# Plain writes for the gate scatters of the first head in a PEER decoder step

## The reference

```python
q = (tb @ wq).reshape(PEER_BLOCK, PEER_HEADS, 2, PEER_QHALF)
sc = jnp.einsum('thpd,hpnd->thpn', q, keys)
s1, i1 = lax.top_k(sc[:, :, 0], PEER_TOPK)
s2, i2 = lax.top_k(sc[:, :, 1], PEER_TOPK)
...
top_s, top_p = lax.top_k(cand, PEER_TOPK)
eidx = jnp.take_along_axis(cidx, top_p, axis=-1)
g = jax.nn.softmax(top_s, axis=-1)
act = jax.nn.gelu(jnp.einsum('td,thkd->thk', tb, u_tab[eidx]))
w = (g * act)
return jnp.einsum('thk,thkd->td', w, v_tab[eidx])
```

## Time and profile before

| | |
|---|---|
| Runs before the change | 3567.2, 3569.97, 3570.47 us, median 3569.97 |
| Span of the profiled execution | 3562.4 us |
| The profiled execution's own time | not listed apart; the median lies 7.6 us above the span |
| Mean granted TensorE clock | 0.976 of full speed |
| Scatters at the edited line | 384, median 1547 ns, from 700.5 to 1429.8 us |
| Barrier between the two blocks | about 1445.3 us |

### The profile page before, as it was taken

One profiled execution on the slowest core, in us unless ns is written; L12 is line 12 of the kernel. 1 busy time (PEld: TensorE's weight loads), 2 busy tenths in 40 slices (PEclk: granted clock), 3 DMA queues, 4 the chain that ended last, 5 costly groups with the idle time before them and its releaser, 6 DMA issues.

```text
span 3562.4 us, 41298 instructions
## 1 busy us (share of the span) xinstructions
PE 3364.8 (94%) x12551; PEld 1749.8 (49%) x12551; DVE 2602.8 (73%) x5430; ACT 840.4 (24%) x1785; POOL 2055.5 (58%) x1620
## 2 busy tenths in 40 slices
PE   8999799899999977899999999999999999999898
PEld 5676464444444445544444444444444444444343
DVE  3444574567877854678888888888888888888784
ACT  2333561344344454211111111111111111111021
POOL 0000100188888888477777777777777677777540
PEclk9999899999999978899999999999999999999999
DMA  4000633588899986899999999999999999999961
GB/s 149 30 29 15 240 143 105 160 201 220 217 221 225 231 211 164 294 395 406 407 405 397 406 403 403 405 387 407 406 403 401 396 390 407 405 405 399 340 218 42
DMA packets 410615, 1023.34 MB, mean 287 GB/s; under 512 B 93965, under 2 KB 130030, under 8 KB 406834
## 3 DMA queue, kind: packets, MB, share of 16 engines
q0 software_dynamic: 221184, 604.27, 46.7%
q1 hardware_dynamic: 175138, 394.69, 31.8%
q10 hardware_dynamic: 14096, 22.02, 1.7%
HBM read 972.05 MB, written 48.77 MB: 287 GB/s over the span
## 4 chain that ended last, share of the span: by engine, by line
DMA 19%; POOL 17%; PE 10%; issue 7%; DVE 6%; ACT 0%; DVEq 0%; SPq 0%; ACTq 0%; POOLq 0%
DMA u<-in_peer_u,idx_all 18%; POOL v L2210 9%; POOL u L2202 8%; PE e_b L2103 3%; PE e_b L2135 2%; PE q_banks L2135 2%; DVE u L2220 1%; DVE facc L2248 1%; PE e_b L2364 1%; DMA w_room<-x_scratch 1%; DVE k_room L2150 0%; PE e_b L2089 0%; PE e_b L2352 0%; DVE wq L2248 0%; DVE w_room L2434 0%
## 5 line engine op out<-in xcount | busy, mean ns | idle before, releaser
L2202 POOL DMA_INDIRECT u<-in_peer_u,idx_all x576 | 719.0, 1248 | 401.6 <-DVE act L2220 262.4
L2220 DVE CUSTOM_DVE_ANT_0 u<-u,xb 128x1024 f32<-128x1024 f32 x576 | 704.9, 1224 | 300.0 <-DMA u<-in_peer_u,idx_all 292.3
L2103 PE MATMUL e_b<-wq 128*128 128x512 f32 x2048 | 900.9, 593 | 0.0
L2210 POOL DMA_INDIRECT v<-in_peer_v,idx_all x576 | 699.5, 1214 | 215.5 <-issue 176.9
L1827 POOL DMA_INDIRECT gate_scratch<-e_room,slot_of x384 | 610.9, 1591 | 160.0 <-issue 117.4
L2103 PEld LDWEIGHTS e_b<-wq 128*128 128x128 f32 x2048 | 379.6, 190 | 429.5 <-issue 429.5
L2135 PE MATMUL q_banks<-w_room,e_room 128*128 128x512 f32 x1024 | 456.3, 599 | 17.5 <-DVE k_room L2150 8.8
L2135 PE MATMUL e_b<-w_room,e_room 128*128 128x512 f32 x1024 | 452.7, 595 | 6.3 <-DVE k_room L2150 6.3
L2248 DVE SCALAR_TENSOR_TENSOR facc<-v,w,facc 128x1024 f32<-128x1024 f32 x317 | 406.7, 1283 | 1.4
L2135 PEld LDWEIGHTS q_banks<-w_room,e_room 128*128 128x128 f32 x1024 | 195.7, 192 | 269.0 <-issue 248.2
L2248 DVE SCALAR_TENSOR_TENSOR wq<-v,w,wq 128x1024 f32<-128x1024 f32 x254 | 325.7, 1282 | 0.5
(11 more groups left out here) (406 smaller groups left out, 3820.4 us busy)
## 6 DMA issues: line engine op xcount, KB each, us to landing
wq<-in_peer_u SPq DMA_DIRECT2D x128, 512.0 KB, 9.8
w_room<-in_peer_v SPq DMA_DIRECT2D x128, 512.0 KB, 10.4
w_room<-in_cache_v SPq DMA_DIRECT2D x144, 256.0 KB
w_room<-in_cache_k SPq DMA_DIRECT2D x128, 256.0 KB
gate_scratch<-zeros SPq DMA_DIRECT2D x24, 1024.0 KB, 26.5
wq<-gate_scratch SPq DMA_DIRECT2D x96, 256.0 KB, 16.7
u<-in_cache_k SPq DMA_DIRECT2D x60, 256.0 KB
xb<-in_cache_k SPq DMA_DIRECT2D x60, 256.0 KB
```

Source lines behind the costliest of these rows:

```text
L2103: last = pe.matmul(AQ[c % 2][:, 0:DT], UT[c % 2][:, k, :], x1Td[:, k, :], start=(k == 0), stop=(k == KC - 1))
L2202: pool.indirect_dma_start(u[x % NU], None, a["peer_u"], bass.IndirectOffsetOnAxis(ap=idx_all[:, t, h, j:j + 1], axis=0)).then_inc(s_u[x % ...
L2210: pool.indirect_dma_start(v[y % NV], None, a["peer_v"], bass.IndirectOffsetOnAxis(ap=idx_all[:, t, h, j:j + 1], axis=0)).then_inc(s_v[y % ...
L2220: dve.tensor_tensor_reduce(u[x % NU], u[x % NU], xb[t % 2][:], 1.0, 0.0, ALU.mult, ALU.add, act16[k % 2][:, j:j + 1]).then_inc(s["ufree"], 1)
```

## The change

The scatters of head 0 lose their compute operation: they write the gate over the zero that lies in the plane, where they added it to that zero before. The scatters of heads 1 to 7 still add. All waits, all counts and the order of the transfers stay as they were.

```diff
                 for m in range(NSC):
                     if j == 0:
                         wait(pool, s_gs[m], 16 * TOPK * h)
-                    pool.indirect_dma_start(gate_d[m].rearrange("e (t o) -> (e t) o", o=1),
-                                            bass.IndirectOffsetOnAxis(ap=slot_of[:, m, h, j:j + 1], axis=0),
-                                            gd[:, m, h, j:j + 1], None, compute_op=ALU.add).then_inc(s_gs[m], 16)
+                    words = gate_d[m].rearrange("e (t o) -> (e t) o", o=1)
+                    slots = bass.IndirectOffsetOnAxis(ap=slot_of[:, m, h, j:j + 1], axis=0)
+                    if h == 0:
+                        pool.indirect_dma_start(words, slots, gd[:, m, h, j:j + 1], None).then_inc(s_gs[m], 16)
+                    else:
+                        pool.indirect_dma_start(words, slots, gd[:, m, h, j:j + 1], None,
+                                                compute_op=ALU.add).then_inc(s_gs[m], 16)
```

## The result

The changed kernel takes 3623.46 us (median of four runs, 3616.34 to 3632.66), against 3568.97 us before (four runs, 3567.20 to 3570.47). The ratio is 1.0165, with a 95% interval from 1.0144 to 1.0187. It is slower by 54.5 us, where no change was forecast. The profiled execution took 3632.66 us with a span of 3630.9 us, 68.5 us more than the span of before; it is the slowest of the four. In each of these four runs the time lies 1.8 us above the span, so most of the 7.6 us that the prediction put around the span were probably the difference between one run of before and another. The 54.5 us compare medians and are the measure of the loss; the 68.5 us compare two single executions.

The account below looks back on a forecast made before the run. The prediction took PE and SP to bound the first block, with POOL's scatters hidden. Terms of 0 for POOL, queues and PE's work gave 3562.4 + 0 + 7.6 = 3570.0 us, range 3563.5 to 3576.5.

Parts of the forecast that it names:

- What bounds the kernel: End of first block: SP, waiting for PE's query products, holds the barrier; POOL is idle there for 16.39 us.
- The price on POOL: Head 0: a plain scatter takes about 1.5 us, range 0.94 to 2.40, against 1.547 for an adding one.
- Bound by PE and SP, whatever head 0 does between 0.94 and 1.74 us a scatter: First block: head 0's scatter time stays hidden, so the kernel's time is unchanged at 3570; chance 0.87.
- 0 in PE's work: Term of the sum: the edit adds or saves 0 us in PE's work.
- SP still waits for PE until 1436.2: End of first block: SP's wait for PE's query products ends at 1436.2, even with POOL's saving at its largest.
- None of the four: The rivals: late page loads, earlier second block (3541, chance 0.01), slower plain scatter, unchanged POOL time (3570, within the 0.87).
- slow path rival: Head 0: plain scatters cost POOL more, deciding from 1.74 us each; at 2.40, +31.6 us, 3602; chance 0.05.
- queues rival: Sample's attention: page loads are truly late, hidden by PE's waits for ScalarE; up to -11 us, 3559; chance 0.05.
- No gate wait takes it back: Heads 1 and 2: gates written at 745.7 and 833.7 are early enough, so all 29.1 us saved reach POOL's end.
- head 1's start: Sign on POOL: head 1's scatters begin between 763 and 792 us.
- the last scatter's end: Sign on POOL: the first block's last scatter ends between 1400 and 1430 us.
- q_banks near 1436: Sign before the barrier: SP's wait at L2467 is still ended by PE's query products near 1436 us.

Follow-up runs that it names:

- e4: The kernel before with the scatters of head 0 left out: 3564.45 against 3560.54 us, ratio 1.0007 [0.9994, 1.0020].
- e11: The changed kernel with only the first 15 of head 0's 48 scatters plain, the other 33 adding: 3585.62 us against 3560.50 before, ratio 1.0073.
- e9: The changed kernel with head 0's scatters replaced by 48 plain indirect reads of 16 single words, back to back: 3618.50 us against 3560.50 before, ratio 1.0163.
- e8: The changed kernel with head 0's 48 transfers reading 128 words from the planes' computed places instead of writing: 3618.84 us against 3560.03 before, ratio 1.0168.
- e14: Head 0's scatters replaced by 48 direct loads of 16 rows of 32 bytes, issued by POOL: 3562.11 us against 3561.77 before, ratio 0.9992.
- e16: Head 0's scatters replaced by 48 indirect loads of 16 rows of 32 bytes, named by a list: 3559.14 against 3560.79 us before, ratio 1.0002.
- e18: Head 0's scatters replaced by 48 direct loads of 16 single words, issued by POOL back to back: 3562.31 us, ratio 1.0003 to the kernel before.
- e17: Head 0's scatters replaced by 48 indirect loads of 16 neighbouring pieces of two words (8 bytes): 3625.20 against 3561.29 us before, ratio 1.0181.
- e7: The changed kernel with head 0's plain scatters sent to 128 neighbouring words of a spare tensor: 3617.29 us against 3560.03 before, ratio 1.0163.
- e1: The changed kernel with one clear of 300 words on POOL after each plain scatter: 3563.54 against 3560.54 us before, ratio 1.0008.
- e3: The changed kernel with only head 0's 16 scatters to the first plane plain, the others adding: 3561.79 us, ratio 1.0005 to the kernel before.

## Why the prediction was wrong

**What bounds the kernel.** Right. The first block is ended by PE and SP, POOL's scatters are hidden, and POOL's idle time at the barrier was the thing to read; e4 shows it directly. The 48 additions of head 0, taken away altogether, give nothing.

**The price on POOL.** The value taken, 1.5 us, was wrong, and the lower end, 0.94, was nearly the measured one: 0.958 us, the price of the gathers. The choice "nearest in shape and direction" lost against "nearest in kind". The saving on POOL was 48 x (1.547 - 0.958) = 28.3 us (POOL's busy total fell by 27.8), within the forecast 0 to 29. By itself this error would have cost the forecast nothing.

**The step that failed** is the sentence "Bound by PE and SP, whatever head 0 does between 0.94 and 1.74 us a scatter", with the last zero of the sum behind it, "0 in PE's work". It treated POOL as an engine that touches the others only through its semaphores and its queue, so that a shorter POOL could at worst be useless. The runs show that the pace of POOL's transfers is itself an input to everyone else. At 1.85 us a start it did nothing; at 1.26 us it stopped PE, VectorE, ScalarE and SP for the length of the stretch. "SP still waits for PE until 1436.2" became 1503.8, with the same products of PE to wait for. The term that was put at 0 measured 54.5 us, about the 60.5 us of the 48 plain scatters (700.6 to 761.1), and e11 shows that it goes with the number of them. The prediction costed the low end as a gain that is hidden. It was the dangerous end.

**The rivals.** None of the four has the mechanism. The slow path rival had the sign: it looked for a plain scatter over 1.74 us that is late at the barrier, and the loss came from one of under 1.4 us that makes all the others late. The queues rival had it the other way round: it expected emptier queues to help PE. The queues did become emptier, 0.02 of their time from 740 to 760, since SP stood waiting for PE and issued nothing. The sign of a faster POOL was taken from its own chain alone.

**The gate waits.** "No gate wait takes it back" was computed with VectorE's times of before. Those times moved: head 1's gates came at 801.9 in place of 745.7, and POOL itself waited 41.1 us for them.

**The signs.** Of the signs that the prediction named, the wait of 16 us or more at the barrier and the fall of POOL's busy total by 0 to 29 us came true; head 1's start (802.2, not 763 to 792), the last scatter's end (1444.7, not 1400 to 1430) and q_banks near 1436 did not. A last scatter that ends after 1439 and a late third plane read were listed as the signs of a slow plain scatter. Both came, without it: the plain one was the faster.

**Two rules that were quoted.** The prediction quoted the Trainium skill ("Perfetto Trace Analysis", section on the DMA instruction of GpSimd) for a profiled time that is spent on descriptors, and took from it that adding would not change that time. The time changed from 1547 to 958 ns with the same 128 words; the packets changed too, from 144 to 32, and in e9 an eighth of the words shortened it only to 0.85 us. So the rule may hold, but the step from "same words" to "same list" did not. The Trainium skill's rule on writes below 512 bytes ("DMA: Bandwidth & Descriptors", Specifications) has no part in the loss that a run shows: e8, which only reads DRAM, loses as much as the writes. Whether the chip does what the rule says, no run here tells.

**What stays open.** The conditions are shown: the indirect form, small pieces (4 and 8 bytes, not 32), and starts less than some 1.45 us apart. What they have in common inside the chip is not. Memory writes, the spread of addresses (for transfers of 128 words), words per us, DMA engine time, semaphore steps per us and the early page loads are each excluded by a run. That the path for hand-overs and issues is occupied is an inference from what is slow; the profile names only "remote", or nothing at all. The size between 8 and 32 bytes at which it ends was not looked for; the pieces of e14, e16 and e18, the three without loss, also lay 4 KB apart, those of e9 and e17 side by side; among transfers of 128 single words the spread made no difference (e7 side by side, e8 spread). For transfers of 16 pieces, spacing was not changed by itself, so that part of the size and form conditions rests on e7 and e8. Nor was an adding form under 1.4 us to be had. No version beats the kernel before: with the scatters hidden, e1 and e3 come back to its time and no further.

## What to carry to other kernels

When an edit makes a hidden engine faster, ask what its pace does to the others before writing down zero: a row at the new pace is needed, and in this trace no long run of POOL transfers under 1.85 us apart with small pieces existed. In a list of indirect transfers of a few bytes from POOL, look at the time from start to start; under about 1.45 us everything else may stand still, and a short clear or adding transfers between them, larger pieces (32 bytes here), or the direct form removed that. A stretch in which all engines but one go idle at once and none has more to do, with waits of several us that end "remote" or "issue", is the sign of it. A merged row of SP's queue is no measure of its issues: it holds SP's waits too, so its waits have to be read beside it.

## What the runs showed of the hardware that was not expected

A plain indirect transfer of 128 words takes POOL 0.96 us and is recorded as 32 packets; the adding form takes 1.55 us and 144 packets. Sixteen words take 0.85 us, so the time hardly goes with the words; 32 adding words take 1.33 us.

48 indirect transfers of single or double words, back to back at 1.15 to 1.27 us, stop the rest of the core: waits of ScalarE of 6 to 10 us that end "remote", 2.7 and 4.2 us for SP from the end of a wait to the load behind it. At 1.37 us PE still did 23.3 us of work in 60 and the loss was as large; at 1.49 us there was none to be told from noise. Direct transfers by POOL at 0.475 us and indirect ones of 32 bytes at 1.15 us do not stop it.

In such a standstill PE's granted clock falls to 0.50 (1.2 GHz). In the changed kernel it averaged 0.75 in the 20 us in which PE was busy for 6.2, 0.50 in the two in which it was busy for 2.6 and 1.6, and still 0.71 from 760 to 780 and from 780 to 800 us, where PE was busy for 12.7 and 19.4.
